# The input projection's order: attention's middle steps between the v, c, x and b blocks, the convolution's half of w_out first, and three modulation rows moved behind the expert queries

## The reference, cut to what matters

```python
mod = silu(c) @ w_ada + b_ada                     # 6 vectors of 1024: 12 rows of 512
h = rms_norm(x, norm1_w) * (1 + scale1) + shift1
q, k, v, cb, cc, cx, iq, ik, iw = split(h @ w_in) # q, k, v, cb, cc, cx, iq: 512 columns each
q, k = rms_norm per head (8 heads of 64)
# indexer (iq, ik, iw): the 64 best keys of each query; the others are masked
o = softmax(q @ k.T * scale, masked) @ v          # y_attn
y_conv = cb * causal_conv3(cc * cx)               # 512 channels
y_mix = concat(rms_norm(y_attn), rms_norm(y_conv))
x = x + gate1 * (y_mix @ w_out)
h2 = rms_norm(x, norm2_w) * (1 + scale2) + shift2
# experts: queries h2 @ peer_wq, the 16 best of 128 x 128 experts per head,
# rows of peer_u and peer_v fetched by index, x = x + gate2 * their sum
```

## Time and profile before

| what | us |
|---|---|
| three runs | 1923.06, 1923.08, 1928.8 (median 1923.08) |
| the profiled execution | 1919.89 |
| its span, first to last instruction | 1918.1 |
| TensorE busy in the span | 1667.7 (87%) |
| VectorE busy | 1232.5 (64%) |
| ScalarE busy | 710.6 (37%) |
| GpSimd busy | 445.8 (23%) |
| mean granted TensorE clock | 0.934 |

### The profile page before, as it was taken

How to read it: one execution, slowest core, us unless ns; L and a number is a source line. 1 busy time by engine, 2 the same in 40 slices (tenths; PEclk the granted TensorE clock), 3 DMA queues, 4 the chain that set the end, 5 groups by cost and what they waited for, 6 DMA issues and landing times.

```text
span 1918.1 us, 25541 instructions
## 1 busy us (share of the span) xinstructions
PE 1667.7 (87%) x9860; PEld 1327.1 (69%) x9860; DVE 1232.5 (64%) x1970; ACT 710.6 (37%) x1284; POOL 445.8 (23%) x343
## 2 busy tenths in 40 slices
PE   5997889288888888875989589999999999999997
PEld 3895686156565655552634179998899896889997
DVE  3774469588878876757667755565336546665554
ACT  3443343333323222113222257655434441344442
POOL 1660541244434443433445300000000000000000
PEclk8997889699889999897999899999999999999998
DMA  8446646999999999999999976544524551335442
GB/s 351 150 173 272 263 176 284 423 369 423 412 420 422 421 414 421 417 423 406 396 422 422 406 282 233 236 165 179 220 88 176 185 200 55 131 134 220 183 167 91
DMA packets 57572, 538.52 MB, mean 281 GB/s; under 512 B 6384, under 2 KB 6512, under 8 KB 7152
## 3 DMA queue, kind: packets, MB, share of 16 engines
q1 hardware_dynamic: 20592, 268.48, 35.8%
q0 software_dynamic: 36864, 268.45, 33.8%
HBM read 535.86 MB, written 1.05 MB: 280 GB/s over the span
## 4 chain that ended last, share of the span: by engine, by line
PE 59%; DMA 22%; DVE 10%; issue 6%; ACT 3%; POOL 1%; POOLq 0%; DVEq 0%; ACTq 0%; SPq 0%
PE psum L429 58%; DMA arena<-in_experts,idx_stage 19%; DVE arena L1747 1%; DMA ring<-in_w_ada 1%; DMA ring<-in_w_in 1%; POOL arena L967 1%; DVE h_t L1425 1%; DVE h_t L1413 0%; DVE ring_r L1336 0%; DMA ring<-in_peer_wq 0%; DVE rstd L1392 0%; ACT small L1244 0%; ACT small L1240 0%; DVE arena_r L1401 0%; DVE arena L1837 0%
## 5 line engine op out<-in xcount | busy, mean ns | idle before, releaser
L1336 DVE TENSOR_TENSOR ring_r<-ring,ring_r 128x1024 fp32r<-128x1024 f32 (+1 forms) x240 | 287.0, 1207 | 274.5 <-ACT ring_r L1000 273.5
L429 PE MATMUL psum<-arena,small 128*128 128x512 f32 x544 | 302.3, 687 | 160.6 <-ACT small L1244 160.4
L1740 DVE CUSTOM_DVE_ANT_0 arena<-arena 128x1024 f32<-128x1024 f32 x256 | 313.7, 1225 | 187.0 <-DMA arena<-in_experts,idx_stage 181.4
L429 PE MATMUL psum<-small_r,ring_r 128*128 128x256 f32 x2304 | 417.8, 281 | 7.0 <-DVE h_t_r L1419 7.0
L967 POOL DMA_INDIRECT arena<-in_experts,idx_stage x256 | 303.4, 1185 | 380.6 <-DVE arena L1747 173.4
L429 PEld LDWEIGHTS psum<-small_r,ring_r 128*128 128x128 f32 x2304 | 360.9, 188 | 14.9 <-issue 14.2
L429 PE MATMUL psum<-h_t_r,ring_r 128*128 128x256 f32 x1152 | 328.7, 285 | 0.0
L429 PE MATMUL psum<-arena_r,ring_r 128*128 128x256 f32 x2208 | 325.6, 280 | 3.1 <-DVE arena_r L1401 2.8
L1000 ACT ACTIVATE ring_r<-ring 128x1024 fp32r<-128x1024 f32 (+1 forms) x240 | 246.3, 1041 | 214.1 <-PE psum L429 174.3
L429 PEld LDWEIGHTS psum<-arena,small 128*128 128x128 f32 x544 | 110.7, 213 | 294.0 <-ACT small L1244 176.5
L429 PEld LDWEIGHTS psum<-arena_r,ring_r 128*128 128x128 f32 x2208 | 289.8, 189 | 3.8 <-DVE arena_r L1401 3.2
(11 more groups left out here) (226 smaller groups left out, 1515.3 us busy)
## 6 DMA issues: line engine op xcount, KB each, us to landing
ring<-in_w_ffn SPq DMA_DIRECT2D x33, 2048.0 KB, 7.7
ring<-in_w_in SPq DMA_DIRECT2D x31, 2048.0 KB, 7.5
ring<-in_w_ada SPq DMA_DIRECT2D x28, 2048.0 KB, 8.6
ring<-in_w_ffn SPq DMA_DIRECT2D x24, 1408.0 KB, 6.3
ring<-in_w_out SPq DMA_DIRECT2D x4, 2048.0 KB, 7.5
ring<-in_peer_wq SPq DMA_DIRECT2D x4, 2048.0 KB, 7.5
ring<-in_p_ret SPq DMA_DIRECT2D x4, 2048.0 KB, 7.4
arena<-in_experts,idx_stage POOLq DMA_INDIRECT x256, 12.7
```

Source lines behind the costliest of these rows:

```text
L429: return nc.tensor.matmul(o, a, b, start=first, stop=last)
L1336: nc.vector.tensor_tensor(whole(i, ring_r), whole(i, ring), upper(i).bitcast(F32), ALU.subtract).then_inc(lo_made, 1)
L1740: step(nc.vector.tensor_tensor_reduce(u, u, h2[:, n // PER_TILE, :], 1.0, 0.0, ALU.mult, ALU.add, dots[:, n % 8, s:s + 1]), sem("dots"))
```

## The change

1. **Slabs and TensorE's order.** After kss: v, the first half of cc, the logits, the second half of cc, cx, row 4, transposes of block 0, cb, row 5, transposes of block 1, row 6, pv0 and pv1, the convolution's squares, pv2 and pv3, the attention's squares, wo0 and wo1, rows 7 and 8, wo2 and wo3, row 9, the squares of norm 2, rows 10 and 11, then the expert queries. Rows 12, 13 and 14 stand behind them, ahead of row 15. The first slab of peer_wq is now loaded into the slot of the second slab of w_out (before: of the first).
2. **wo0** takes the convolution's four blocks first, then the attention's.
3. **Roots.** The sums of squares of q, k and of the two norms of the mix are read out of PSUM by ScalarE, which takes the root with scale and epsilon; VectorE takes the reciprocal after it. The scaling by VectorE and one handshake per norm are gone.
4. **VectorE's order.** Logits, softmax and both normalisations stand ahead of the convolution.
5. **ScalarE's order.** It follows TensorE's; the upper parts of w_out's first two pieces are made after row 6, those of the next two after the root of the attention's norm and ahead of the copies of the mix; rows 7 and 8 stand between the squares of x 3 and 4, row 9 behind the last of them.
6. **Places.** The probabilities of block 1 lie in `h_t`, the transposed ones in the indexer's space, the attention's squares behind the convolution's.

```diff
-    first = (mods[:4] + w_in(0) + [("w_idx", 0, KD * 136)] + w_in(1) + w_in(2) + w_in(4) + w_in(5) + w_in(6) + w_in(3)
-             + mods[4:13] + out_proj + mods[13:15] + peer(0) + peer(1) + peer(2) + peer(3) + mods[15:GAP])
+    first = (mods[:4] + w_in(0) + [("w_idx", 0, KD * 136)] + w_in(1) + w_in(2) + w_in(3) + w_in(4) + w_in(5) + mods[4:5]
+             + w_in(6) + mods[5:7] + out_proj[:1] + mods[7:9] + out_proj[1:] + mods[9:12] + peer(0) + peer(1) + peer(2) + peer(3)
+             + mods[12:GAP])
...
@@ TensorE
-            split_feature("cc", 2, h1_hi, h_lo_1, "act")
-            split_feature("cx", 2, h1_hi, h_lo_1, "dve")
-            split_feature("cb", 2, h1_hi, h_lo_1, "dve")
             split_token("v", 1, h_hi_1, h_lo_1)
+            split_feature("cc", 1, h1_hi, h_lo_1, "act")
 
             pe.wait_ge(sem("qk_ready"), 4)
...
-            mod_steps(4, 6, False)
-            squares("conv", sq1, KA)
-            for t in range(NT):
+            split_feature("cc", 1, h1_hi, h_lo_1, "act", start=1)
+            split_feature("cx", 2, h1_hi, h_lo_1, "dve")
+            mod_steps(4, 5, False)
...
+            turn_probs(0)
+            split_feature("cb", 2, h1_hi, h_lo_1, "dve")
+            mod_steps(5, 6, False)
+            turn_probs(1)
+            mod_steps(6, 7, False)
             pe.wait_ge(*emptied("pt1_3"))
...
-            mod_steps(8, 10)
-            squares("att", sq1, KA)
-            mod_steps(10, 13)
-            split_feature("wo", 4, lambda k: h_hi_1[:, k, :], y_mix_lo, "dve",
-                          need={k: (sem("y_split"), (k + 2) if k < KA else 1) for k in range(KD)})
+                if j == 1:
+                    squares("conv", sq1, KA, "act")
+            squares("att", sq1[:, KA:KD, :], KA, "act")
+            need = {k: (sem("y_split"), (k + 2) if k < KA else 1) for k in range(KD)}
+            split_feature("wo", 2, lambda k: h_hi_1[:, k, :], y_mix_lo, "dve", need=need, order=[*range(KA, KD), *range(KA)])
+            mod_steps(7, 9, False)
+            split_feature("wo", 2, lambda k: h_hi_1[:, k, :], y_mix_lo, "dve", start=2)
+            mod_steps(9, 10)
             squares_by_block("n2", sq1, KD - 2)
-            mod_steps(13, 15)
+            mod_steps(10, 12)
...
-            mod_steps(15, GAP)
+            mod_steps(12, GAP)
...
@@ ScalarE
-            for a in range(2):
+            for a, tag in ((0, "q"), (1, "k")):
                 for i in range(2):
-                    root(flat(raw_sq[:, a, 2 * i:2 * i + 2, :]))
-                    ahead(f"{('cx', 'cb')[a]}{i}")
+                    drain(nc.scalar.activation(flat(raw_sq[:, a, 2 * i:2 * i + 2, :]), take(f"{tag}ss{i}"), ACT.Sqrt,
+                                               bias=eps, scale=1.0 / HD))
...
+            for i in range(2):
+                copy_out(f"cc{i}", flat(gate_c[:, 2 * i:2 * i + 2, :]))
+            for t in range(NT):
+                exp_probs(t)
+                ahead(f"cx{t}")
+            mod_steps(4, 5, False)
+            split_until(first_out - 1)
+            copy_probs(0)
+            mod_steps(5, 6, False)
+            copy_probs(1)
+            mod_steps(6, 7, False)
+            split_until(first_out + 1)
+            act.wait_ge(sem("y_conv"), 1)
+            square("conv", sq1, y_conv, KA)
...
+                if j == 1:
+                    norm_root("conv", ATT)
+            act.wait_ge(drained["act"], taken[0])
+            square("att", sq1[:, KA:KD, :], y_att, KA)
             act.wait_ge(sem("y_mix"), KA)
-            act.wait_ge(drained["act"], taken[0])
-            square("att", sq1, y_att, KA)
-
             nc.scalar.activation(flat(h_hi_1[:, KA:KD, :]), flat(y_mix[:, KA:KD, :]), ACT.Copy).then_inc(sem("y_hi"), 1)
-            root(rstd[:])
+            norm_root("att", ATT)
+            split_until(first_out + PIECES - 1)
             for j in range(KA):
                 act.wait_ge(sem("y_mix"), KA + j + 1)
                 nc.scalar.activation(h_hi_1[:, j, :], y_mix[:, j, :], ACT.Copy).then_inc(sem("y_hi"), 1)
-            split_until(first_out + PIECES - 1)
-            mod_steps(10, 13)
-            norm_hi("n2", 1, mod1[:, 24:32], [f"wo{i}" for i in range(4)], sq1, h_hi_2)
-            mod_steps(13, 15)
+            norm_hi("n2", 1, mod1[:, 24:32], [f"wo{i}" for i in range(4)], sq1, h_hi_2,
+                    between={KA: lambda: mod_steps(7, 9, False), KD: lambda: mod_steps(9, 10)})
+            mod_steps(10, 12)
...
@@ VectorE, q and k
-                    root(f"{tag}ss{i}", rs, BANK, HD)
+                    v.wait_ge(*emptied(f"{tag}ss{i}"))
+                    step(nc.vector.reciprocal(rs, rs))
...
+            def rooted_norm(tag):
+
+                v.wait_ge(*emptied("ss_" + tag))
+                step(nc.vector.reciprocal(rstd[:], rstd[:]))
+
+            logits(0)
+            logits(1)
+            normalise(0)
+            normalise(1)
```

More of the change, by code:

```diff
@@ L502, in three, with pair_by_block @@
                 return mm(o, w_lo, a_hi, False, last)
-            def pair_by_block(o, need, hi, lo, name):
+            def pair_by_block(o, need, hi, lo, name, order):
                 two = [next_piece(j) for j in range(2)]
-                for k in range(KD):
+                for n, k in enumerate(order):
                     if k in need:
@@ L510, in pair_by_block, with split_feature @@
                     last = [three(o[:, j * L:(j + 1) * L], w_hi[:, k, :], w_lo[:, k, :], hi(k), lo[:, k, :],
-                                  k == j == 0, k == KD - 1 and j == 1) for j, (_, w_hi, w_lo) in enumerate(two)]
+                                  n == j == 0, n == KD - 1 and j == 1) for j, (_, w_hi, w_lo) in enumerate(two)]
                 piece_end(last[0])
                 piece_end(last[1], name)
-            def split_feature(tag, count, hi, lo, who, kb=KD, need=None, start=0):
+            def split_feature(tag, count, hi, lo, who, kb=KD, need=None, start=0, order=range(KD)):
                 need = need or {}
@@ L521, in split_feature @@
                     if len(need) == KD and kb == KD:
-                        pair_by_block(o, need, hi, lo, f"{tag}{n}")
+                        pair_by_block(o, need, hi, lo, f"{tag}{n}", order)
                         continue
@@ L565, in split_feed_forward @@
                         if need:
-                            pair_by_block(o, need, h_hi_of, h_lo, name)
+                            pair_by_block(o, need, h_hi_of, h_lo, name, range(KD))
                             continue
@@ L1058, in mod_steps, with norm_hi @@
                     mod_turned(m1 - 1)
-            def norm_hi(tag, m, shift, names, sq=sq2, hi=h_hi, row=None):
+            def norm_hi(tag, m, shift, names, sq=sq2, hi=h_hi, row=None, between={}):
                 for k in range(KD):
+                    if k in between:
+                        between[k]()
                     if names:
```

70 lines of the change are left out of this document (29 added, 41 removed).

## The result

The changed kernel takes 1930.31 us (median of 13 runs, 1925.3 to 1933.96) beside 1926.09 us (median of 13 runs) for the kernel before, timed alongside. The ratio is 1.003, with a 95% interval of 1.0019 to 1.0042: 3.7 to 8.1 us slower, 5.8 in the middle. The forecast was 8.7 slower, 1932 us; its 8.7 lies 0.6 above the interval. The profiled execution took 1930.31 us (span 1928.5).

A forecast was written before the change was run, and what follows sets the result against it. The expert stage was taken as bound by its DMA bytes, the front by TensorE's waits and a chain around norm 2. Tail +14.7 and front -6 gave +8.7 us: 1932 us on 1923.1, range 1926 to 1937.

The forecast's parts named there:

- The tail, +14.7: Behind the expert queries: three moved slabs at 4.9 us each delay context slabs and expert rows by 14.7 us.
- The holes: Gaps in DMA traffic at 386 to 390 and near 910 us, worth 3.9 and 3.8; expected to move along, unfilled.
- the rival in which they swallow the slabs: Expert stage: both DMA gaps take up the slabs, stage pays only 7, not slower, 1924 us; chance 0.13.
- choice of experts is the bound: VectorE's 68.5 us choice sets the expert stage's start and pace; only the front counts, -6 to -14, 1913 us; chance 0.10.
- The rival of a starved start: Start of expert stage: first four batches come 16 late, a longer hole adds 1 to 6, 1936 us; chance 0.10.
- The front's balance: TensorE up to the last w_out pair: fewer rows, less idle and half clock, less new waits; end 232.5 becomes 211.2.
- The three new idle times: TensorE waits before the logits (+5.2), the convolution's and attention's squares (+2.4), and the attention's half of wo0 (+4.5).
- three new spells at half clock: TensorE after the new idle times: some 14 us at half clock, half of it lost, +7.
- The meeting of VectorE and GpSimd: VectorE's q and k products slow beside GpSimd's subtractions, +3.4 for four; two of the attention norm's four products wait.
- The milder outcome: Attention's norm: VectorE's products win the port first, third idle loses nothing, front's sum 3 to 5 us less.
- The chain around norm 2: Peer slab issued at 211.2, landing 7.6, then 14.4 (+3.8 new) to the reciprocal: 233.2, 6.3 earlier than 239.50.
- The rival in which all waits go as laid out: TensorE's front: GpSimd does not hold up VectorE, front gains 12 to 14.5, total +1.7, 1925 us; chance 0.17.

The follow-up runs named there:

- e1: Changed kernel, but the slabs of the moved rows 12 to 14 bring only the first 512 of 4096 words per partition; 1930.06 us.
- e9: Changed kernel, but the slabs of rows 19 to 21 bring only the first 512 of 4096 words per partition; 1920.14 us.
- e2: Kernel before, with only rows 12 to 14 moved behind the peer queries, loads and computation, without the new order; 1936.61 us.
- e5: Changed kernel, but ScalarE copies the upper halves for w_out's second blocks after its four copies of the mixed attention; 1925.44 us.
- e3: Changed kernel, but ScalarE's copies of the first peer query slab's upper half stand behind norm 2's last block; 1915.42 us.
- e10: Kernel before, with ScalarE's copies of the first peer query slab's upper half moved behind norm 2's last block; 1925.35 us.
- e6: Changed kernel, but both blocks of c run on TensorE ahead of the attention logits instead of one on each side; 1922.53 us.
- e7: Changed kernel, but the slabs of rows 15 to 17 bring only the first 512 of 4096 words per partition; 1924.37 us.
- e4: The e3 kernel, with rows 12 to 14 (slabs, TensorE's rows, ScalarE's copies) back ahead of the peer queries; 1916.88 us.

## Why the prediction was right, and where it was not

**The tail, +14.7.** Measured 13.8 between the two profiles and 14.2 with the rows alone. Its size was right: all kernels with four slabs of rows behind the full point have a stretch of 831.8 to 835.2, all with seven full ones 848.3 to 849.5. Its step was half wrong: I charged the three moved slabs. They land in cheap places under the queries (e1: no gain), and three others take the dear ones (e9: 10.3 of 12.9). The sum did not notice, since a slab is a slab. Whoever had acted on my sentence would have cut the wrong bytes. The pace of the rows was as said: TensorE's last six rows start 4.9 apart, all released by DMA,

```profile
319.86 2.42 PE L430 MATMUL psum<-ring,cols 128*32 128x512 f32 x16 [1.43 <-DMA ring<-in_w_ada]
324.76 3.50 PE L430 MATMUL psum<-ring,cols 128*32 128x512 f32 x16 [0.69 <-DMA ring<-in_w_ada]
...
344.40 3.06 PE L430 MATMUL psum<-ring,cols 128*32 128x512 f32 x16 [2.04 <-DMA ring<-in_w_ada]
```

while `mod21` is copied 14.2 us later than before (351.00 against 336.84), where I had said 9.

**The holes.** They moved along and the first kept its size (5.0 and 4.8 us, where I had priced 3.9), so the rival in which they swallow the slabs is out. The regime fills at 304.5 (I said 306). The rival "choice of experts is the bound" is out too: e9 left every row's steps in place and took bytes away, and gained 11.6. The rival of a starved start asked for a longer hole and a tail over 14.7; neither was there.

**The front's balance, 211.2 for the end of the last w_out pair.** It ended at 213.8; without the 2.8 us of the opening, 211.0. The three new idle times were 4.6, 2.3 and 5.2 (4.1 and a 1.1 in front of the convolution's half), against 5.2, 2.4 and 4.5. Of the three new spells at half clock two came, with 12.8 us of TensorE's work in them instead of 14. That this fits so closely is partly luck: terms of both signs met, and e2 shows that one of them, the three rows' TensorE work as a gain of its own, is none in the old order, where TensorE waits that time for GpSimd instead.

**The meeting of VectorE and GpSimd.** The products of q and k took 2.46, 1.76, 2.29 and 2.13 us beside GpSimd's subtractions, 0.75 alone: 5.6 us more for the four, where I had taken 3.4. The attention's took 5.01 for four, and e5, which only moves the subtractions away, brings 2.05. That is what the Trainium skill says in "SBUF — State Buffer", section "SBUF: two separate sides": the two engines shut each other out of a shared port. The trace agrees, with these numbers. The milder outcome, in which VectorE's products win the start, did not come.

**The chain around norm 2.** I gave 7.6 + 14.4 = 22.0 us from the peer slab's issue to the reciprocal; it took 21.8 (213.9 to 235.7), with ScalarE waiting for the slab as said. But the working names only +3.8 for it, the steps that are new inside the chain. Before, the reciprocal stood 7.0 us behind the end of the last w_out pair (232.5 to 239.5), in my sum 22.0. The 15.0 between the two are in the sum, and most of them, the slab's later issue, never got a line or a rival of their own. Against a kernel without the wait the measured price is 14 to 15 us (e3), as much as the tail's three slabs, and before the change it was nothing that the runs can tell (e10). The forecast's total was right by its sum, but one of the two reasons for a slower kernel was a wait that I had described and not priced apart.

**The total.** -3.4 + 13.8 = +10.4 by the profiles, +7.6 without the 2.8 of the opening, 5.8 (3.7 to 8.1) by the runs, 8.7 forecast. The rival in which all waits go as laid out (+1.7) lies below the interval.

## What to carry to other kernels

Before you charge a moved transfer to the place where it now stands, write down which transfers are issued at each freed slot: moving one pushes all behind it along, and the price is paid by the one that falls out of the last cheap place. When an order gets shorter, price every wait that stood hidden behind the old length, above all an in-order engine's wait for a transfer with unrelated work queued behind it: here one such wait was worth some 15 us in one order and nothing that could be told in the other. And take a wait of a few microseconds on TensorE with what it does to the clock behind it: the 4.6 us in front of the logits were worth 6.2 to 7.7.

## What the runs showed of the hardware that I had not expected

- A wait of TensorE goes on costing when it is over, and not the same in each execution. With 4.6 us of idle in front, the 32 products of the logits took 6.51 us in two profiles and 5.06 or 5.07 in five; without the idle they took 3.44 in all three. The granted clock between 120 and 124 was 0.50 (1.2 GHz) in the changed kernel and 1.00 (2.4 GHz) in e6.
- The half-clock spell at 64 to 72 us in the profile of the changed kernel stands where nothing was changed; it made 2.8 us there, as much as many an edit here, and the end of k scatters from 92.2 to 97.1 over the thirteen profiles. A place is best counted from another one just ahead of the edit.
- Cutting 7/8 of the bytes of three slabs gave 0, 4.1 or 10.3 us of stretch for the same 12.9 us of transfer, by their place in the queue alone (e1, e7, e9).
- VectorE's eight additions of the shift to h2, with one input from SBUF each beside the shift's column, took 2.19 us in the changed kernel, where GpSimd stood, and 12.9 us in e4 beside five of its subtractions: not only products with two inputs are slow beside GpSimd.
- The 72 to 31 of the earlier trace rows goes with the size of the packets and not with their number: the two queues moved 112 and 107 packets there, of 16.4 and 7.1 KB in the mean.
